# A decoder layer on one core: triangular solves placed on all four 64x64 tiles, decay sums shifted, values centred while they are turned

## The chip, the core and the metric

The kernel runs on one core of a Trainium2 chip: TensorE (matrix products into PSUM), VectorE, ScalarE and GpSimd (elementwise work), SyncE (issues the DMAs). The metric is the device time of one execution in microseconds (us), the median of the runs. Everything is float32. Products of large weights run as "split" products: a value is kept as a rounded high part and a low part, and hi x hi, hi x lo and lo x hi are summed.

## The reference

One layer for 256 tokens of width 2048. What bears on the change is the RWKV-7 mixer (16 heads of 64 columns):

```
w = -softplus(-(w0 + tanh(w_d) @ w_up)) - 0.5
decay = exp(-exp(w))                      # = exp(-DECAY * sigmoid(logit))
S_t = S_{t-1} * w_t + (S_{t-1} @ -kk_t) (kk_t * a_t)^T + v_t k_t^T ;  y_t = S_t r_t
mean = y.mean(-1); var = square(y - mean).mean(-1)      # per head
y = (y - mean) * rsqrt(var + eps) * gn_gain + gn_bias
out = (y + sum(r * k * r_k) * v) * g
```

Beside it stand a differential attention of 8 heads, one output projection, a LayerNorm, a squared-ReLU MLP (8192 wide) and a second LayerNorm.

## The kernel before

The program has five instruction streams, one for each engine, each written out in its order by hand. Semaphores tie them; there is no scheduler. Weights arrive as 1 MB slabs (128 x 2048 float32) in four rotating buffers `stage`. For each slab ScalarE rounds a high half (`hi`, tile `whi`), VectorE subtracts it for the low half (`lo`, tile `wlo`), and TensorE multiplies. Two slabs of halves are held, so `hi` of a slab waits until TensorE has used the slab two before it, and `lo` waits for `hi`.

The stages in order: the LoRA columns; decay and rate terms; the r, k, v columns of the projection (24 slabs, four rounds of three column groups); the attention's q and k (16 slabs, `q` = 0 to 15, in which the triangular solve is woven in); the attention's v with scores and softmax; transposes and chunk products; state passing; the group norm among output-projection products (`out_rows`); LayerNorm; MLP (128 slabs, some 730 us).

**Decay sums.** Tokens are in chunks of 64. For each of 8 blocks of 128 columns TensorE multiplies the decay sigmoids (`sig`) with two triangular 0/1 matrices side by side, 256 columns for each of two token tiles: the strict one gives the sum before a token, the inclusive one the sum up to it. The eight blocks pass through four PSUM banks (4 to 7). ScalarE takes exponentials of both (`kr`, with `e` = 0 and 1) and of the negated inclusive sum (`e2`). Between the sigmoids of the rates (`bt`) and the exponentials ScalarE also makes `hi` of slab 4 (`G_MIX + 1`). The rotary sines follow the exponentials.

**The solve.** There are 32 units (16 heads x 2 token tiles), each with two chunks, one in each half of the partitions. Groups of 8 units are solved in two streams (`st` 0 and 1) and two turns. For a turn, level 0 makes the matrices from PSUM (`AT`, and the starts of the inverse `TM` and its transpose `TT`); levels 1 to 5 each take an x product (factor `AT` times `TM`, 16 products of 64x64 over 64), a mask on VectorE into `XM`, a t product (32 products, `XM` with `TM`'s transpose both ways; 16 at level 5), and a copy back on ScalarE. `solve_at` puts level 0 at slab q = 1 and q = 8, and levels 1 to 5 at q = 3 to 7 and 10 to 14. Inside a slab the x products stand ahead of k steps 1 and 3, the t products ahead of steps 5 and 7.

A product whose inputs lie in partition half r and whose output lies in half o uses one quarter (64x64 tile) of the array, written (r to o) here. `halves_of` uses only (0 to 1) and (1 to 0), alternating; the t products of levels 1 to 4 use all four. A float32 product is two TensorE instructions, so `x32` in a row is 16 products.

**Turning.** `turned(i, bk)` makes eight 128x128 transposes; i = 2 and 3 are the values `v` (`krv` blocks 16 to 23 into `vtm`), i = 0 and 1 the keys, 4 and 5 `bt`, 6 and 7 `ki`.

**Group norm.** When y is complete (`copied(g)`, g = 0 to 3), TensorE sums each head with a block matrix of ones (`mean`, 128x512), VectorE subtracts the mean (`centred`), ScalarE squares, TensorE sums the squares, and root, reciprocal, spreading and gain follow.

Of the kernel before, what the change touches and what calls it, by code (L numbers as in the profile page):

```python
# [8 lines left out]
ALU = mybir.AluOpType  # L9
# [7 lines left out]
P = 128  # L17
# [88 lines left out]
def build(nc, t):  # L106

    ctx = ExitStack()
    with ctx:
# [9 lines left out]
        def sem(name):  # L119
# [43 lines left out]
        attT += [at("attT7", 22, [P, 3 * P])]  # L163
        otok = at("otok", 23, [P, TT_, RW])
# [5 lines left out]
        TM = at("TM", 16, [P, UNITS, C])  # L170
        TT = at("TT", 18, [P, UNITS, C])
        XM = [at("XM0", 24, [P, 8, C], byte=6144), at("XM1", 12, [P, 8, C], byte=5120)]

# [84 lines left out]
            "level_x", "level_x_masked", "level_products", "level_done"))  # L258
        s_rdx, s_rdm = sem("read_out_products"), sem("read_out_masked")
# [10 lines left out]
        s_mean, s_cen, s_gsq, s_var, s_sd, s_gn, s_gate, s_yg = (  # L270
            sem("gn_means"), sem("gn_centred"), sem("gn_squares"), sem("gn_vars"), sem("gn_roots"),
# [99 lines left out]
        def _(sp):  # L371
# [29 lines left out]
            sp.wait_ge(s_itemd, 2 * NB)  # L401
# [55 lines left out]
        def _(pe):  # L457
# [69 lines left out]
            for n in range(2 * NB):  # L527
                b, bk = n % NB, 4 + n % 4
                if n < 4:
                    pe.wait_ge(s_sig, n + 1)  # L530
                else:
                    pe.wait_ge(s_itemd, n - 3)
                if n < NB:
                    mm(ps[:, bk, 0:S], aup[64:128, P * b:P * b + P], wa[64:128, :]).then_inc(s_item, 1)
                else:
# [39 lines left out]
            def halves_of(bk, a0, b0):  # L575

                for c0 in range(2):
                    for j in range(4):
                        for c, jj, bank in ((c0, j, bk), (1 - c0, 4 + j, bk + 1)):
                            rows_ = chunk_rows(c)  # L580
                            last = mm(ps[chunk_rows(1 - c), bank, C * j:C * j + C], a0[rows_, jj, :], b0[rows_, jj, :])
                return last

            def level_x(st, turn, lev):
# [8 lines left out]
                else:  # L593
# [4 lines left out]
                    last = halves_of(bk, at_group(s), group(TM, s))  # L598
                last.then_inc(s_px[st], 1)

            def level_t(st, turn, lev):
                s, bk = STREAM[st][turn], 4 + 2 * st
                xm, tt = XM[st], group(TT, s)
                pe.wait_ge(s_xm[st], 6 * turn + lev + 1)
                if lev == 5:
                    last = halves_of(bk, xm, tt)
                else:
                    for j in range(8):
                        for r, out, bank, a0, b0 in ((0, 1, 0, tt, xm), (1, 0, 0, tt, xm), (0, 0, 1, xm, tt), (1, 1, 1, xm, tt)):
                            rows_ = chunk_rows(r)  # L610
                            last = mm(ps[chunk_rows(out), bk + bank, C * j:C * j + C], a0[rows_, j, :], b0[rows_, j, :])
# [134 lines left out]
            turned_read(0)  # L746
            turned(2, 0)
# [196 lines left out]
            def mean(g):  # L944
                pe.wait_ge(s_yc, g + 1)
                if g >= 2:
                    pe.wait_ge(s_cen, g - 1)
                mm(ps[:, g % 2, :], BD, yf[:, 2 * g:2 * g + 2, :]).then_inc(s_mean, 1)

# [150 lines left out]
        def _(act):  # L1100
# [48 lines left out]
            for n in range(2 * NB):  # L1149
                b, bk = n % NB, 4 + n % 4  # L1150
                if n == NB:
                    hi(G_MIX + 1, G_MIX + 1)
                act.wait_ge(s_item, n + 1)
                if n < NB:
                    A(bt[:, b, :], ps[:, bk, 0:S], ACT.Sigmoid, bias=col(V_A0, b)).then_inc(s_itemd, 1)
                else:
                    A(kr[:, b, :, :, :].rearrange("p a e q -> p (a e q)"), ps[:, bk, :], ACT.Exp, scale=-DECAY)
                    A(e2[:, b, :].rearrange("p (a q) -> p a q", a=TT_),
                      ps[:, bk, :].rearrange("p (a e q) -> p a e q", a=TT_, e=2)[:, :, 1, :],
                      ACT.Exp, scale=DECAY).then_inc(s_itemd, 1)  # L1160

            act.wait_ge(s_ang, 9)
            A(sinb[:, :], angt[0][:, :], ACT.Sin).then_inc(s_sin, 1)
            A(cosb[:, :], angt[2][:, :], ACT.Sin).then_inc(s_sin, 1)
# [6 lines left out]
            for j in range(NB // 2):  # L1171
                for c in range(3):
                    m = 3 * j + c
                    g = G_MIX + 2 * m
                    hi(g + 2, g + 2)
                    if c == 1:
# [899 lines left out]
```

## Time and profile before

| | us |
|---|---|
| median of 3 runs (1288.81, 1294.73, 1295.5) | 1294.73 |
| the profiled execution, own time | 1291.21 |
| its span | 1289.2 |
| TensorE matrix products busy | 1251.6 (97%) |
| TensorE weight loads busy | 1051.9 (82%) |
| VectorE / ScalarE / GpSimd busy | 756.4 / 574.7 / 72.1 |
| mean granted TensorE clock | 0.994 of full speed |

The span is the time from the first to the last instruction; the execution's own time is 2.0 us longer. All times inside the rows are counted from the span's start. `L459` is the helper through which nearly every matrix product is made, `L1102` the helper of every ScalarE activation, `L1449` the low half of a slab, so that the tile names tell which work it is.

### The profile page before, as it was taken

What the parts mean: (1) busy time and instruction counts of PE and PEld (TensorE: products, weight loads), DVE (VectorE), ACT (ScalarE), POOL (GpSimd) and SP (SyncE); (2) the same over time, 40 slices, a digit from 0 to 9 for tenths busy, and PEclk for the clock granted to TensorE, in tenths of its full rate; (3) what the DMA queues carried; (4) which work ended last, traced back from release to release, by engine and by line L of the source; (5) the groups of instructions that cost most, each with busy time, mean ns of one, the idle gap of its engine ahead of it and who ended that gap; (6) DMA issues with size and microseconds to landing.
All of it is one profiled execution on the core that took longest, in us unless ns stands there. A gap on an engine that the chain in (4) does not pass through costs nothing.

```text
span 1289.2 us, 23229 instructions
## 1 busy us (share of the span) xinstructions
PE 1251.6 (97%) x9624; PEld 1051.9 (82%) x9624; DVE 756.4 (59%) x797; ACT 574.7 (45%) x614; POOL 72.1 (6%) x42
## 2 busy tenths in 40 slices
PE   6999999999999999999999999999999999999995
PEld 6788888888778768888888888888888888888884
DVE  5478777454677245776555555555655555655557
ACT  4754444454665233433443334433444444444443
POOL 0021112000000000038000000000000000000000
PEclk9999999999999999999999999999999999999998
DMA  9254565232340243834555555555565555555541
GB/s 337 99 203 165 194 212 185 100 129 100 131 164 5 101 164 104 295 123 164 195 193 181 183 191 195 195 183 183 191 258 195 195 188 188 190 188 192 195 163 65
DMA packets 33505, 221.88 MB, mean 172 GB/s; under 512 B 4621, under 2 KB 5005, under 8 KB 7582
## 3 DMA queue, kind: packets, MB, share of 16 engines
q1 hardware_dynamic: 33438, 220.88, 49.5%
q8 instruction: 54, 0.88, 0.3%
q14 instruction: 13, 0.11, 0.0%
HBM read 218.77 MB, written 2.10 MB: 171 GB/s over the span
## 4 chain that ended last, share of the span: by engine, by line
PE 54%; DVE 1%; ACT 0%; issue 0%; DVEq 0%
PE ps L459 54%; DVE xres L1950 0%; DVE xres L1948 0%; DVE stats L1838 0%; DVE xres L1837 0%; ACT xres L1102 0%; DVE moments L1841 0%; DVE moments L1848 0%; ACT moments L1102 0%; DVE moments L1847 0%; DVEq L1831 0%
## 5 line engine op out<-in xcount | busy, mean ns | idle before, releaser
L1449 DVE TENSOR_TENSOR wlo<-stage,whi 128x2048 fp32r<-128x2048 f32 x186 | 436.0, 2344 | 387.7 <-ACT whi L1102 387.4
L459 PE MATMUL ps<-acts,whi 128*128 128x512 f32 (+1 forms) x1792 | 613.5, 391 | 15.3 <-DVE wlo L1449 13.1
L1102 ACT ACTIVATE whi<-stage 128x2048 fp32r<-128x2048 f32 x194 | 371.4, 1916 | 497.5 <-PE ps L459 494.3
L459 PE MATMUL ps<-acts,wlo 128*128 128x256 f32 (+1 forms) x1744 | 485.1, 278 | 0.0
L459 PEld LDWEIGHTS ps<-acts,whi 128*128 128x128 f32 x1792 | 333.7, 188 | 89.7 <-issue 20.1
L459 PEld LDWEIGHTS ps<-acts,wlo 128*128 128x128 f32 x1744 | 330.4, 189 | 1.9 <-issue 1.9
L459 PE MATMUL ps<-whi,shi 128*128 128x512 f32 x504 | 197.9, 393 | 0.0
L459 PE MATMUL ps<-wlo,shi 128*128 128x512 f32 x504 | 196.5, 390 | 0.0
L459 PE MATMUL ps<-whi,slo 128*128 128x512 f32 x504 | 196.2, 389 | 0.0
L459 PEld LDWEIGHTS ps<-whi,shi 128*128 128x128 f32 x504 | 94.5, 188 | 26.4 <-issue 6.1
L459 PEld LDWEIGHTS ps<-wlo,shi 128*128 128x128 f32 x504 | 94.6, 188 | 20.2
L459 PEld LDWEIGHTS ps<-whi,slo 128*128 128x128 f32 x504 | 94.7, 188 | 18.1
L459 PE MATMUL ps<-whi,oshi 128*128 128x512 f32 x128 | 53.2, 416 | 0.0
L459 PE MATMUL ps<-whi,oslo 128*128 128x512 f32 x128 | 50.4, 394 | 0.0
L459 PE MATMUL ps<-wlo,oshi 128*128 128x512 f32 x128 | 50.4, 394 | 0.0
L1803 DVE TENSOR_TENSOR slo<-hid,shi 128x512 fp32r<-128x512 f32 x64 | 43.8, 685 | 0.0
L459 PE MATMUL ps<-whi,acts 128*128 128x512 f32 x128 | 41.0, 402 | 0.0
L1102 ACT ACTIVATE shi<-hid 128x512 fp32r (+1 forms) x64 | 39.2, 613 | 1.1 <-PE ps L459 1.1
L1533 DVE TENSOR_TENSOR hs<-ps,hs 128x512 f32<-128x512 f32 x20 | 13.6, 679 | 44.5 <-ACT hs L1102 44.4
L1102 ACT ACTIVATE hs<-ps 128x512 f32<-128x512 f32 x20 | 12.0, 599 | 51.4 <-PE ps L459 51.4
L1988 POOL TENSOR_TENSOR acts<-x1f,acts 128x512 fp32r<-128x512 f32 x6 | 9.7, 1620 | 363.9 <-ACT acts L1102 363.9
L459 PEld LDWEIGHTS ps<-whi,oshi 128*128 128x128 f32 x128 | 24.2, 189 | 7.0 <-issue 2.0
(215 smaller groups left out, 996.9 us busy)
## 6 DMA issues: line engine op xcount, KB each, us to landing
stage<-w_ff SPq DMA_DIRECT2D x128, 1024.0 KB, 4.9
stage<-w_in SPq DMA_DIRECT2D x51, 1024.0 KB, 5.0
stage<-w_out SPq DMA_DIRECT2D x16, 1024.0 KB, 5.0
xstage<-xT SPq DMA_DIRECT2D x4, 512.0 KB, 7.2
xres<-x SPq DMA_DIRECT2D x1, 2048.0 KB, 7.9
gain<-ln_gain SPq DMA_DIRECT2D x2, 1024.0 KB, 6.9
bias<-ln_bias SPq DMA_DIRECT2D x2, 1024.0 KB, 9.0
out<-xres SPq DMA_DIRECT2D x8, 256.0 KB, 2.1
```

Of the source, the lines that this page charges most:

```text
L459: return pe.matmul(out, lhsT, rhs, start=start, stop=stop, skip_group_check=True)
L1102: return act.activation(out, in_, func, **kw)
L1449: TTn(wlo[k0 % NHL][:, :], stage[k0 % NST][:, :], f(whi[k0 % NHL][:, :]), ALU.subtract).then_inc(s_lo, 1)
L1533: TTn(hs[:, :, :], banks(2 * (m % 2), 2, 0, S), hs[:, :, :], ALU.add).then_inc(s_psum, 1)
L1803: TTn(slo[h][:, :, :], src, f(shi[h][:, :, :]), ALU.subtract).then_inc(s_alo, 1)
L1988: PT(actlo[:, ks, tok(a)], x1f[:, ks, tok(a)], f(acthi[:, ks, tok(a)]), ALU.subtract).then_inc(s_x1l, 1)
```

## The change

Four things are edited.

1. Decay sums: only the inclusive sums are made, four banks of two blocks each, 16 products of 128 columns. `kr` with `e` = 0 is taken from the same sums, read one column to the left; its first column in each chunk is set to 1 by a VectorE `memset`. There are three ScalarE exponentials for two blocks. Both halves of slab 4 are made on VectorE, and the sines are moved behind `hi` of slab 5.
2. Solve: units 0 to 3 of a group keep their output in the opposite half, units 6 and 7 in their own half, units 4 and 5 swap sides from level to level. The x products and the level-5 products go in squares of four that use all four tiles. Units 4 and 5 need their factor in both halves, so VectorE copies it (`AF`) at level 0. The t products of levels 1 to 4 write another layout, which ScalarE's two copies follow.
3. Values: `turned` 2 and 3 multiply by `centre` (identity minus 1/64 in each head's block) rather than transpose, so that y comes out centred; `mean` and `centred` are gone.
4. ScalarE makes `hi` of output slab 3 after the four squares, and the products of output slab 2 stand together.

```diff
@@ solve placement
+        def side_a(u, c, lev):
+            return c ^ (lev - 1) % 2 if u in (4, 5) else c
+        def side_s(u, c, lev):
+            return 1 - c if u < 4 else side_a(u, c, lev)
@@ decay sums, TensorE
-            for n in range(2 * NB):
-                b, bk = n % NB, 4 + n % 4
...
-                        last = mm(ps[:, bk, 256 * a:256 * a + 256], sig[:, a, P * b:P * b + P],
-                                  cst[:, C_SU:C_SU + 2 * P])
-                    last.then_inc(s_item, 1)
+            for p in range(NB // 2):
+                pe.wait_ge(s_itemd, 5 + p)
+                for b in (2 * p, 2 * p + 1):
                     for a in range(TT_):
+                        o = 256 * (b % 2) + P * a
+                        last = mm(ps[:, 4 + p, o:o + P], sig[:, a, P * b:P * b + P], IU)
+                last.then_inc(s_item, 1)
@@ solve, TensorE
-            def halves_of(bk, a0, b0):
-
-                for c0 in range(2):
-                    for j in range(4):
-                        for c, jj, bank in ((c0, j, bk), (1 - c0, 4 + j, bk + 1)):
-                            rows_ = chunk_rows(c)
-                            last = mm(ps[chunk_rows(1 - c), bank, C * j:C * j + C], a0[rows_, jj, :], b0[rows_, jj, :])
+            SQUARES = [[(u, c) for c in range(2) for u in (j, 4 + j)] for j in range(4)]
+
+            def x_products(st, s, bk, lev):
+                a0, b0 = at_group(s), group(TM, s)
+                for square in SQUARES:
+                    for u, c in square:
+                        a = side_a(u, c, lev)
+                        left = a0[chunk_rows(a), u, :] if a == c else AF[st][chunk_rows(a), u - 4, :]
+                        last = mm(ps[chunk_rows(side_s(u, c, lev)), bk + u // 4, C * (u % 4):C * (u % 4) + C], left,
+                                  b0[chunk_rows(a), u, :])
+                return last
+
+            def last_products(st, s, bk):
+                xm, tt = XM[st], group(TT, s)
+                for square in SQUARES:
+                    for u, c in square:
+                        rows_ = chunk_rows(side_s(u, c, 5))
+                        last = mm(ps[chunk_rows(c), bk + u // 4, C * (u % 4):C * (u % 4) + C], xm[rows_, u, :], tt[rows_, u, :])
+                return last
@@ values, TensorE
-                            last = pe.transpose(ps[:, bk + k, o:o + P],
-                                                TURNED_SRC[i // 2](4 * (i % 2) + 2 * k + b2, a), ID)
+                            if i // 2 == 1:
+                                last = mm(ps[:, bk + k, o:o + P], src, centre[:, :])
+                            else:
+                                last = pe.transpose(ps[:, bk + k, o:o + P], src, ID)
@@ group norm, TensorE
-            mean(0)
             pe.wait_ge(s_yc, 2)
-            for g in range(1, 4):
-                out_rows(G_OUT + 2, (g - 1,))
-                mean(g)
-            out_rows(G_OUT + 2, (3,))
+            out_rows(G_OUT + 2, range(4))
@@ decay exponentials, ScalarE
+                A(kr[:, two, :, 1, :].rearrange("p b a q -> p (b a) q"), ps[:, 4 + p, :].rearrange("p (m q) -> p m q", q=P),
+                  ACT.Exp, scale=-DECAY)
+                A(kr[:, two, :, 0, :].rearrange("p b a (c q) -> p (b a) c q", c=2)[:, :, :, 1:C], chunks[:, :, :, 0:C - 1],
+                  ACT.Exp, scale=-DECAY)
+                A(e2[:, two, :].rearrange("p b q -> p (b q)"), ps[:, 4 + p, :], ACT.Exp, scale=DECAY).then_inc(s_itemd, 1)
@@ slab 4, VectorE
-            lo(G_MIX + 1, G_MIX + 1)
+            dve.memset(kr[:, :, :, 0, 0::C].rearrange("p b a c -> p (b a) c"), 1.0)
+            g = G_MIX + 1
...
+            dve.tensor_copy(whi[g % NHL][:, :], stage[g % NST][:, :]).then_inc(s_hi, 1)
+            lo(g, g)
@@ level 0, VectorE
-                        last = dve.copy_predicated(by_head(group(TT, s))[out], mask(over8(M1T)[out]), bb[rows_])
+                        dve.copy_predicated(tt[out, 0], mask(over8(M1T)[out, 0]), bb[rows_, 0])
+                    dve.wait_ge(s_ax, 2 * turn + st + 1)
+                    for c in range(2):
+                        last = dve.tensor_copy(AF[st][chunk_rows(1 - c), :, :], at_group(s)[chunk_rows(c), 4:6, :])
@@ centring, VectorE
+            STT(centre[:, :], BD, -1.0 / HD, ID, ALU.mult, ALU.add).then_inc(s_centre, 1)
@@ group norm, VectorE
-                STT(y512, ps[:, g % 2, :], -1.0 / HD, y512, ALU.mult, ALU.add).then_inc(s_cen, 1)
```

The order of the instructions shows it at three places. On TensorE, the decay sums before (`sig` are the decay sigmoids, `cst` the triangular constants):

```order
L459 MATMUL ps<-wa_148,aup_63 128x256 [waits decay_sigmoid] x4
L459 MATMUL ps<-wa_148,aup_63 128x256 [waits rate_or_cumsum_done] x4
L459 MATMUL ps<-cst_144,sig_64 128x256 [waits rate_or_cumsum_done]
L459 MATMUL ps<-cst_144,sig_64 128x256
L459 MATMUL ps<-cst_144,sig_64 128x256 [waits rate_or_cumsum_done]
```

and the same place changed:

```order
L471 MATMUL ps<-wa_150,aup_63 128x256 [waits decay_sigmoid] x4
L471 MATMUL ps<-wa_150,aup_63 128x256 [waits rate_or_cumsum_done] x4
L471 MATMUL ps<-cst_146,sig_64 128x128 [waits rate_or_cumsum_done]
L471 MATMUL ps<-cst_146,sig_64 128x128 x3
L471 MATMUL ps<-cst_146,sig_64 128x128 [waits rate_or_cumsum_done]
```

Sixteen products of 256 columns in eight pairs become sixteen of 128 columns in four groups of four.

On VectorE, level 0 of one stream at q = 1, before:

```order
L1591 COPY_PREDICATED AT01_108<-cst_144,ps 128x512 [waits eyes_loaded_first_groups,level_x_stream0]
L1592 COPY_PREDICATED TM_110<-levc_107,ps 128x512
L1595 COPY_PREDICATED TT_111<-levc_107,ps 64x512 x2
```

and changed:

```order
L1637 COPY_PREDICATED AT01_109<-cst_146,ps 128x512 [waits eyes_loaded_first_groups,level_x_stream0]
L1638 COPY_PREDICATED TM_TT_111<-levc_108,ps 128x512
L1639 COPY_PREDICATED TM_TT_111<-levc_108,ps 128x256
L1642 COPY_PREDICATED TM_TT_111<-levc_108,ps 64x256 x2
L1645 COPY AF0_114<-AT01_109 64x128 [waits level_factors_ready]
L1645 COPY AF0_114<-AT01_109 64x128
```

Two operations of 512 columns become three of 256, and two copies of 128 columns are added.

On TensorE where y is complete, before (`yf` is y, `cst` the ones of a head):

```order
L459 MATMUL ps<-yf_132,cst_144 128x512 [waits y_copied]
L459 MATMUL ps<-whi1_54,oshi0_84 128x512 [waits diff_hi_ready,lo_ready,diff_lo_ready,hi_ready,y_copied]
L459 MATMUL ps<-whi1_54,oslo0_86 128x512
L459 MATMUL ps<-wlo1_56,oshi0_84 128x512
L459 MATMUL ps<-whi1_54,oshi0_84 128x512
L459 MATMUL ps<-whi1_54,oslo0_86 128x512
L459 MATMUL ps<-wlo1_56,oshi0_84 128x512
L459 MATMUL ps<-yf_132,cst_144 128x512 [waits y_copied]
```

and changed (`gsq` are the squares, the first product behind the slab):

```order
L471 MATMUL ps<-whi1_54,oshi0_84 128x512 [waits diff_hi_ready,lo_ready,diff_lo_ready,hi_ready,y_copied]
L471 MATMUL ps<-whi1_54,oslo0_86 128x512
L471 MATMUL ps<-wlo1_56,oshi0_84 128x512
L471 MATMUL ps<-gsq_136,sumg_133 16x256 [waits gn_squares,y_copied,norm_windows_loaded]
L471 MATMUL ps<-gsq_136,sumg_133 16x256
```

The four products on `yf` are gone (of the slab's 24 products the first three are shown).

## Rows read from the trace of the kernel before

**Rows 1.** Page, part 1: busy us (share of the span) x instructions of each engine.

```profile
PE 1251.6 (97%) x9624; PEld 1051.9 (82%) x9624; DVE 756.4 (59%) x797; ACT 574.7 (45%) x614; POOL 72.1 (6%) x42
```

**Rows 2.** Waits of PE: us in total, times, longest us.

```profile
PE ps L459 <- DVE wlo L1449: 13.1, 4, 11.5
```

**Rows 3.** Timeline, decay sums: start us, us, engine, line, op, count [idle before <-releaser].

```profile
34.99 0.29 DVE L1507 TENSOR_SCALAR angt<-angt 128x256 f32<-128x256 f32 x1
37.46 3.72 PE L459 MATMUL ps<-cst,sig 128*128 128x256 f32 x16
39.87 2.29 DVE L1449 TENSOR_TENSOR wlo<-stage,whi 128x2048 fp32r<-128x2048 f32 x1 [4.59 <-ACT whi L1102]
...
42.08 3.72 PE L459 MATMUL ps<-cst,sig 128*128 128x256 f32 x16 [0.90 <-ACT e L1102]
...
45.45 0.58 PE L459 MATMUL ps<-acts,whi 128*128 128x512 f32 x1
...
51.54 1.91 ACT L1102 ACTIVATE whi<-stage 128x2048 fp32r<-128x2048 f32 x1 [2.12 <-PE ps L459]
```

**Rows 4.** Timeline of PE, the attention's 128-column products and transposes.

```profile
391.90 2.84 PE L459 MATMUL ps<-vd,attT 128*128 128x128 f32 x24
394.58 1.04 PE L698 MATMUL ps<-cst,kr 128*128 128x128 f32 x8
395.45 1.04 PE L698 MATMUL ps<-cst,krv 128*128 128x128 f32 x8
...
397.39 1.09 PE L698 MATMUL ps<-cst,krv 128*128 128x128 f32 x8 [0.57 <-ACT kttm L1102]
398.90 1.06 PE L698 MATMUL ps<-cst,bt 128*128 128x128 f32 x8 [0.42 <-DVE vtm L1686]
```

**Rows 5.** Timeline of PE, solve: level 0's products at q = 1, x products at q = 3 and 4.

```profile
197.30 0.69 PE L459 MATMUL ps<-bt,kr 64*64 64x64 f32 x32
197.81 0.65 PE L459 MATMUL ps<-kr,bt 64*64 64x64 f32 x32
198.39 0.50 PE L459 MATMUL ps<-acts,whi 128*128 128x512 f32 x1
...
209.15 1.15 PE L459 MATMUL ps<-TM,AT 64*64 64x64 f32 x32
210.23 0.50 PE L459 MATMUL ps<-acts,whi 128*128 128x512 f32 x1
...
219.90 1.15 PE L459 MATMUL ps<-TM,AT 64*64 64x64 f32 x32
```

**Rows 6.** Window of one t product, PE alone: length, busy (x), PEclk, DMA, GB/s.

```profile
214.52:215.62 1.10, 1.10 (x66) 1.00 0.90 194
```

**Rows 7.** Lines by form, PE, 200 to 340 us: busy us, mean ns | idle before.

```profile
L459 PE MATMUL ps<-acts,whi 128*128 128x512 f32 x230 | 87.3, 416 | 1.3 <-DVE wlo L1449 1.3
```

**Rows 8.** Timeline of DVE, level 0 at q = 1.

```profile
199.34 0.75 DVE L1591 COPY_PREDICATED AT<-cst,ps 128x512 f32<-128x512 int32 x1
...
200.73 1.53 DVE L1595 COPY_PREDICATED TT<-levc,ps 64x512 f32<-64x512 int32 x2
202.29 0.76 DVE L1591 COPY_PREDICATED AT<-cst,ps 128x512 f32<-128x512 int32 x1
```

**Rows 9.** Timeline of ACT and PE, y copied and two head means of the group norm.

```profile
460.61 1.09 ACT L1102 ACTIVATE yf<-ps 128x512 f32<-128x512 f32 x2 [23.20 <-PE ps L459]
...
462.47 1.02 PE L459 MATMUL ps<-yf,cst 128*128 128x512 f32 x2
...
464.71 1.02 PE L459 MATMUL ps<-yf,cst 128*128 128x512 f32 x2
```

**Rows 10.** Windows: length, busy (x) of PE, PEld, DVE, ACT, POOL, PEclk, DMA, GB/s.

```profile
220.00:230.00 10.00, 10.00 (x221) 8.48 (x222) 6.17 (x7) 6.23 (x10) 0.00 (x0) 1.00 0.52 181
...
436.00:440.00 4.00, 2.15 (x144) 2.01 (x138) 1.29 (x2) 1.41 (x1) 0.00 (x0) 1.00 0.08 29
444.50:448.10 3.60, 3.60 (x44) 2.53 (x43) 1.29 (x2) 0.00 (x0) 0.00 (x0) 0.54 0.85 291
```

More of the change, by code:

```diff
@@ L163, in build @@
         attT += [at("attT7", 22, [P, 3 * P])]
+        centre = at("centre", 22, [P, P], byte=1536)
         otok = at("otok", 23, [P, TT_, RW])
@@ L525, in _ @@
                     mm(ps[:, 4 + 2 * a + q, :], wt[:, tok(a)], wup[:, 512 * q:512 * q + 512]).then_inc(s_z, 1)
-            for n in range(2 * NB):
-                b, bk = n % NB, 4 + n % 4
+            for n in range(NB):
                 if n < 4:
@@ new lines, in last_products, with t_products, inverse, transposed @@
+            def last_products(st, s, bk):
[5 more added lines that the diff above has]
+                return last
+            def t_products(st, s, bk, lev):
+                xm, tt = XM[st], group(TT, s)
+                def inverse(u, r):
+                    rows_, out = chunk_rows(r), chunk_rows(1 - r if u < 6 else r)
+                    o = C * u if u < 6 else C * (u - 2)
+                    return mm(ps[out, bk + u // 6, o:o + C], tt[rows_, u, :], xm[rows_, u, :])
+                def transposed(u, r):
+                    rows_, out = chunk_rows(r), chunk_rows(1 - r if u in (4, 5) else r)
+                    o = C * u if u < 4 else C * (u + 2) if u < 6 else C * u
+                    return mm(ps[out, bk + (u not in (4, 5)), o:o + C], xm[rows_, u, :], tt[rows_, u, :])
+                for u in range(4):
+                    inverse(u, 0)
+                    inverse(u, 1)
+                    transposed(u, 0)
+                    last = transposed(u, 1)
+                for u in (4, 5):
+                    for what in (inverse, transposed):
+                        for v in (u, u + 2):
+                            for r in range(2):
+                                last = what(v, r)
@@ L597, in level_x @@
                         pe.wait_ge(s_upd[st], 5 * turn + lev - 1)
-                    last = halves_of(bk, at_group(s), group(TM, s))
+                    last = x_products(st, s, bk, lev)
                 last.then_inc(s_px[st], 1)
@@ L602, in level_t @@
                 s, bk = STREAM[st][turn], 4 + 2 * st
-                xm, tt = XM[st], group(TT, s)
                 pe.wait_ge(s_xm[st], 6 * turn + lev + 1)
[L605 to L611, printed above, removed]
+                last = last_products(st, s, bk) if lev == 5 else t_products(st, s, bk, lev)
                 last.then_inc(s_ptx[st], 1)
@@ L1174, in _ @@
                     g = G_MIX + 2 * m
+                    if m == 0:
+                        act.wait_ge(s_hi, g + 2)
                     hi(g + 2, g + 2)
+                    if m == 0:
+                        sines()
                     if c == 1:
@@ L1204, in level_done @@
                 if lev < 5:
[L1205 to L1206 removed]
+                    o = 8 * C * s
+                    A(TM_TT[:, :, o:o + 256], banks(bk, 2, 0, 256), ACT.Copy)
+                    A(TM_TT[:, :, o + 256:o + 512].rearrange("p t (k q) -> p k t q", k=2),
+                      banks(bk, 2, 256, 512).rearrange("p k (t q) -> p k t q", t=2), ACT.Copy).then_inc(s_upd[st], 1)
                 else:
@@ L1340, in _ @@
             hi(G_OUT + 2, G_OUT + 2)
-            copied(0)
-            copied(1)
-            hi(G_OUT + 3, G_OUT + 3)
-            copied(2)
-            copied(3)
+            for g in range(4):
+                copied(g)
             for g in range(4):
                 squared(g)
+            hi(G_OUT + 3, G_OUT + 3)
             hi(G_OUT + 4, G_OUT + 4)
@@ L1788, in rwkv_lo @@
                 TTn(oslo[1][:, bl, :], yt[:, bl, :], f(oshi[1][:, bl, :]), ALU.subtract).then_inc(s_olo[1], 1)
-            centred(0)
             lo(G_OUT + 3, G_OUT + 3)
-            for g in range(1, 4):
-                centred(g)
             lo(G_OUT + 4, G_OUT + 4)
```

71 lines of the change are left out of this document (32 added, 39 removed).

## The prediction

> **What bounds the kernel now.** I read the busy shares first, then what TensorE waits for, then the timeline at each edited place, TensorE ahead of the engines that serve it. TensorE's products are busy 1251.6 of 1289.2 us, VectorE 59%, ScalarE 45% [rows 1]. TensorE's waits for a low half are 13.1 us in all, of which 11.5 is the one before its first product [rows 2]. So TensorE is the bound nearly everywhere, and a microsecond taken off its stream comes off the end, unless VectorE or ScalarE becomes late. There are three places where TensorE does wait near the edits: 0.90 us at the decay sums for ScalarE's exponentials [rows 3], 1.3 us in the solve, all of it for low halves of slabs [rows 7], and 0.57 and 0.42 us among the turned values [rows 4]. The first shrinks with the edit, in the second every added VectorE operation counts in full, the third can swallow added work. Everything behind the group norm (some 790 us) is not touched and only starts earlier.
>
> **Decay sums.** TensorE starts on them at 37.46 and is on the first projection slab at 45.45 [rows 3]: 7.99 us, which is 32 instructions of 256 columns in two blocks of 3.72 and the wait between. Now there are 16 products of 128 columns, 32 instructions. The pace of such instructions with full weights is in the attention: 24 take 391.90 to 394.58, 0.112 us each [rows 4]. 32 x 0.112 = 3.6 us. All four groups have a free bank once the rates are read, so no wait stands inside. Gain 8.0 - 3.6 = 4.4 us. What must be in time: both halves of slab 4. VectorE is free from 35.3 [rows 3]; the low half takes 2.29 us there, the high half by a copy has no row, and I bound it by 0 and by the same 2.29. Even then both are done by 35.5 + 4.6 = 40.1, and slab 4 is only needed after slab 3, which TensorE begins at 37.5 + 3.6 = 41.1. ScalarE loses a 1.9 us `hi` and keeps its exponentials: twelve of 512 columns against eight of 512 and eight of 256, 6144 columns either way. Its next `hi` (slab 5) waits for TensorE anyway, 2.12 us at 51.54 [rows 3], and the sines are moved behind it, where VectorE needs them only when slab 4 is through. I find nothing late. Bounds of the gain: 4.0 (0.4 of start-up) and 4.4.
>
> **Solve.** An x product is 32 instructions on two tiles and takes 209.15 to 210.23, 1.08 us. What would 32 instructions on four tiles take? Level 0's products use all four: the first 32 take 197.30 to 197.81, 0.51, the second, with the change back to full width, 0.58 [rows 5]. A t product on four tiles, 64 instructions, is 1.10 us [rows 6]: twice the work in the time of one x product. Taking its 1.10 as 64 steps plus about 0.15 for the change over, 32 steps come to 0.63. So 0.58 to 0.63; I take 0.60 and a gain of 0.48 each. There are 2 turns x 2 streams x 5 levels = 20 x products and 4 of level 5 in squares: 24 x 0.48 = 11.5 us (10.8 to 12.0). The t products of levels 1 to 4 keep their count and their four tiles: 0. ScalarE's two copies carry the same elements: 0.
>
> What must be in time here: a slab with solve work shrinks from 10.75 us (209.15 to 219.90, x product to x product [rows 5]) to 9.8. VectorE's mask of stream 1 stands behind a `lo` and ahead of the rotary work, and nothing on TensorE waits for a mask: the view of waits names none, and the only idle time of 200 to 340 us stands before slab products, 1.3 us, for low halves [rows 7]. In 220 to 230 us VectorE is busy 6.2 and ScalarE 6.2 of 10 [rows 10]. Both have about 2 us in hand for each slab, and 0.5 us of it goes before the t products. Cost 0.
>
> Against it stands level 0. VectorE does it in 199.34 to 202.29, 2.95 us for a stream [rows 8], and what follows is the low half for which TensorE waits, at q = 1 to 3 and again at q = 8 to 10; so additions count. Two 512-column operations of 1.53 become three of 256; one 512 is about 0.53 of columns and 0.2 of fixed time by the 0.75 there, so 256 is 0.27 + 0.15 to 0.2, three about 1.3. Two copies of 128 columns have no row: between 0.1 and 0.3 each. Together 1.5 to 1.9 against 1.5: 0 to +0.4, I take +0.1, times 4 = +0.4 us (0 to 1.4).
>
> **Values.** A transpose is one instruction: eight take 394.58 to 395.45, 0.109 each [rows 4]. As products they are two each at 0.112, so eight take 1.79 instead of 0.87. Two calls add 1.8 us of work. The first starts at 395.45 as before and ends 0.9 later; the wait of 0.57 in front of the second goes, then the second adds 0.9, and the wait of 0.42 in front of the turned `bt` goes. 1.84 - 0.57 - 0.42 = 0.85; the copies that ended those waits move by a little with the products, but the last copy of the values was queued behind a reduction on VectorE and hardly moves. I take +0.7 us (0.4 to 1.8). The `centre` tile is one VectorE operation while VectorE waits for TensorE: 0.
>
> The Trainium skill (TensorE: Matmul & The Clock Gate, Terms) says that transpose mode makes float32 four times faster. The trace gives a factor of two, 0.109 against 2 x 0.112 [rows 4]. By the page a product would be 0.44, sixteen would add 5.2 us rather than 1.8, and the gain would be 3.4 us smaller; the rows decide.
>
> **Group norm.** A mean and six slab products take 462.47 to 464.71 = 2.24 us [rows 9]. A mean is two instructions of 512 columns, as much as four of 256, which are 3.72 / 16 = 0.23 each [rows 3], so 0.9, with the tail of the group in it; I take 0.86, which leaves 0.23 for each slab product. Four means: 3.4 us. Behind it the squares must be in time. The four copies of y and the squares on ScalarE no longer wait for VectorE, and slab 3's `hi` stands after them; TensorE has 24 products (5.5 us) of slab 2 to do meanwhile. ScalarE's four copies and four squares, at 1.09 for two [rows 9], are some 4.4 us from 460.6, the `hi` and `lo` of slab 3 are 1.9 and 2.3 more [rows 3]: 469 us. TensorE comes to slab 3 no sooner than 462.5 + 5.5 + 3.7 for the sums of squares (16 instructions of 256 columns) = 471.7. Cost 0; bounds of the gain 2.5, where slab 3 were a microsecond late, and 3.5.
>
> **The sum.** -4.4 - 11.5 + 0.4 + 0.7 - 3.4 = -18.2 us. The profiled execution took 1291.2 us, so 1273.0 by its own clock. It lies between the timed runs of 1288.8 and 1295.5, whose median is 1294.7, so these would give 1276.5. I take the mean of the four executions, 1292.6, as the base: 1274.4, say 1274.5 us. Half a per cent, about what a measurement of this kernel can tell from no change, is 6.5 us: under 1288.3 is faster.
>
> **Rivals.**
> 1. *The squares do not overlap.* The Trainium skill (TensorEngine Tiling, Gotcha 1) says that different row tiles cannot access the same PSUM bank at the same time, and each square sends two row halves into one bank. If TensorE serialised such pairs, an x product would stay at 1.08. For it: the edit does put (0 to 1) and (1 to 0) of one square into one bank, on different output halves. Against it: the t products do so too and run 64 instructions in 1.10 [rows 6]. The gain would be 18.2 - 11.5 = 6.7, time 1286. A chance of 0.06.
> 2. *The level chain becomes the bound.* If the mask or the copy of stream 1 came after its reader in each of the ten slabs, half of the solve's gain would be given back: 12.5 us of gain, 1280. For it: VectorE and ScalarE handle everything in a fixed order behind `hi` and `lo`. Against it: no such wait now, and 2 us in hand. 0.10.
> 3. *TensorE runs out of instructions (slower).* Where the 64x64 products stand densest, 436 to 440 us, TensorE is busy 2.15 of 4.00 us at 144 instructions, with no engine to wait for; after such holes its clock is at the lower level, 1.2 GHz, for most of 3.6 us (granted 0.54) [rows 10]. The new x products put 32 instructions into 0.6 us. If each of the 24 calls met a hole of 1.3 us, that would be +31 and the time 1305; it decides from 18.2 / 24 = 0.76 us a call. Against it: slabs with solve work run 221 instructions in 10 us without a hole [rows 10] and would run 224 in 9.8, and the t products are as dense as the new ones. 0.03.
> 4. *The clock moves.* The same stretch at 444.5 costs 3.6 x (1 - 0.5) = 1.8 us; work ahead of it moves by 16 us, and it may go, or another may come: 1.8 either way, inside the range.
> 5. *The edits do little*, since something hidden holds the old pace at the decay sums and the norm as well: 1288 to 1292, 0.03.
>
> **Numbers.** The forecast has 0.78, its own range 1268 to 1281: gains from 15 to 20.5, and bases from 1288.8 to 1295.5. Rival 2 ends at 1280 to 1283, rival 1 at 1286, rival 3 above 1290. I give 1268 to 1283. Faster: 0.78 + 0.10 + 0.05 of rival 1 = 0.93. Within half a per cent: 0.01 + 0.03 = 0.04. Slower: 0.03.
>
> **What would show it.** Decay sums: 32 instructions of 128 columns in one block of 3.6 us, the first slab product at about 41, no wait between. Solve: the `TM,AT` group of 32 over 0.6 us, distance from one x product to the next of its stream about 9.8 us where it was 10.75; the wait for low halves between 1.3 and 2 us. Values: groups of 16 on `centre`, turned `bt` less than 1 us later against its neighbours. Norm: no products on `yf`, 24 slab products in one piece, `gsq` straight behind. It would be wrong if an x product keeps 1.08 us, if TensorE shows new holes with no releaser, if VectorE's level 0 grows by 0.5 us or more for a stream, or if ScalarE's slab 5 `hi` comes after TensorE's need.

## The result and the profile after

The changed kernel takes 1280.57 us (median of 6 runs, 1276.29 to 1282.53) against 1294.55 for the one before (6 runs): a ratio of 0.989, 95% interval 0.987 to 0.992. Forecast were 1274.5 us, range 1268 to 1283. The profiled execution took 1276.29 us with a span of 1274.5, so the span is 14.7 us shorter than the 1289.2 of before; the forecast was 18.2.

The busy line of the page, which answers to [rows 1]:

```profile
PE 1236.8 (97%) x9632; PEld 1038.0 (81%) x9632; DVE 756.9 (59%) x808; ACT 572.2 (45%) x609; POOL 69.8 (5%) x42
```

TensorE's products are 14.8 us shorter at nearly the same count, and that is the change of the span: TensorE still is the bound. Its waits (us in total, times, longest), beside [rows 2]:

```profile
PE ps L471 <- DVE wlo L1490: 15.0, 3, 11.6
PE ps L471 <- issue: 4.3, 3, 2.1
```

The waits for low halves grew from 13.1 to 15.0 us. The timeline says which ones. First the decay sums, beside [rows 3] (start us, us, engine, line, operation, count, idle before):

```profile
37.26 2.29 DVE L1490 TENSOR_TENSOR wlo<-stage,whi 128x2048 fp32r<-128x2048 f32 x1
...
38.26 3.84 PE L471 MATMUL ps<-cst,sig 128*128 128x128 f32 x32
...
41.85 0.48 PE L471 MATMUL ps<-acts,whi 128*128 128x512 f32 x1
```

One block from 38.26 to 41.85, no wait in it and slab 4's low half done at 39.6. Now TensorE at q = 3, where [rows 5] had the first x product at 209.15:

```profile
206.27 0.47 PE L471 MATMUL ps<-acts,whi 128*128 128x512 f32 x1 [1.96 <-DVE wlo L1490]
...
207.13 0.76 PE L471 MATMUL ps<-TM_TT,AT 64*64 64x64 f32 x32
207.81 0.80 PE L471 MATMUL ps<-acts,whi 128*128 128x512 f32 x1
...
228.27 0.69 PE L471 MATMUL ps<-TM_TT,AT 64*64 64x64 f32 x32
```

Before, TensorE waited 0.45 us for a low half at q = 3 and 0.88 at q = 9; now the second is 1.42 (two rows of the kernel before, then one of the changed kernel):

```profile
208.28 0.47 PE L459 MATMUL ps<-acts,whi 128*128 128x512 f32 x1 [0.45 <-DVE wlo L1449]
...
276.96 0.47 PE L459 MATMUL ps<-acts,whi 128*128 128x512 f32 x1 [0.88 <-DVE wlo L1449]
```

```profile
271.46 0.47 PE L471 MATMUL ps<-acts,whi 128*128 128x512 f32 x1 [1.42 <-DVE wlo L1490]
```

The x product at 228.27 is what was forecast (0.62 us to its successor's start, where it was 1.08), but the one at 207.13 runs behind a wait of 1.96 us, and its neighbour, a slab product of 512 columns, has 0.80 us where 0.40 is usual. The windows show why (length; busy (x) of PE, PEld, DVE, ACT, POOL; PEclk; DMA; GB/s):

```profile
204.00:207.00 3.00, 1.04 (x6) 0.60 (x4) 2.59 (x2) 2.94 (x5) 0.00 (x0) 1.00 0.00 0
207.00:208.00 1.00, 1.00 (x35) 0.76 (x34) 0.96 (x3) 1.00 (x1) 0.00 (x0) 0.81 0.77 131
208.00:209.00 1.00, 1.00 (x3) 0.86 (x4) 1.00 (x2) 0.44 (x1) 0.00 (x0) 0.50 0.87 328
...
211.00:212.00 1.00, 1.00 (x35) 0.89 (x28) 0.76 (x2) 0.00 (x0) 0.00 (x0) 0.98 0.04 16
```

TensorE idled for two of the first three microseconds, and then the granted clock is 0.50, the level of 1.2 GHz, from 208 to 211. Before there is no fall in the solve. The low half comes late because VectorE's level 0 is longer. Here is all of it at q = 1 for stream 0, the copies of stream 1, and GpSimd beside it; [rows 8] is its counterpart:

```profile
195.81 0.75 DVE L1637 COPY_PREDICATED AT<-cst,ps 128x512 f32<-128x512 int32 x1
196.45 0.73 DVE L1638 COPY_PREDICATED TM_TT<-levc,ps 128x512 f32<-128x512 int32 x1
197.09 0.43 DVE L1639 COPY_PREDICATED TM_TT<-levc,ps 128x256 f32<-128x256 int32 x1
197.53 0.93 DVE L1642 COPY_PREDICATED TM_TT<-levc,ps 64x256 f32<-64x256 int32 x2
198.47 1.60 DVE L1645 COPY AF<-AT 64x128 f32<-64x128 f32 x2
...
202.74 0.46 DVE L1645 COPY AF<-AT 64x128 f32<-64x128 f32 x2
```

```profile
197.21 1.29 POOL L2024 TENSOR_TENSOR bt<-bt,e  x1 [0.17 <-POOL kr L2022]
198.47 1.28 POOL L2025 TENSOR_TENSOR ki<-ki,e  x1
```

The same two copies take 1.60 us for stream 0, beside GpSimd's product of `ki`, and 0.46 for stream 1, when GpSimd is through. Taken singly, it is one copy that is long; it ends 0.09 us after the product of `ki` (199.75), and the next takes 0.22:

```profile
198.47 1.37 DVE L1645 COPY AF<-AT 64x128 f32<-64x128 f32 x1
199.85 0.22 DVE L1645 COPY AF<-AT 64x128 f32<-64x128 f32 x1
```

The three predicated copies, which read PSUM, are at 0.43 to 0.93 in both streams. Level 0 of both streams takes 7.42 us (195.81 to 203.23) where it took 5.91: stream 0 has 1.34 us more and stream 1 0.17.

The values go in two blocks on `centre` with no wait before them or before the turned `bt` (beside [rows 4]), and at the group norm ScalarE makes four squares and then `hi` of slab 3 (beside [rows 9]):

```profile
384.60 1.95 PE L471 MATMUL ps<-centre,krv 128*128 128x128 f32 x16
...
386.71 1.95 PE L471 MATMUL ps<-centre,krv 128*128 128x128 f32 x16
388.50 1.04 PE L744 MATMUL ps<-cst,bt 128*128 128x128 f32 x8
```

```profile
451.43 2.21 ACT L1138 ACTIVATE gsq<-yf 128x512 f32<-128x512 f32 x4
453.51 1.93 ACT L1138 ACTIVATE whi<-stage 128x2048 fp32r<-128x2048 f32 x1
```

From marks on TensorE's timeline (before / after): decay sums to slab 3, 7.99 / 3.59 us; decay sums to the first x product, 171.69 / 168.87; from there to the turned values, 186.30 / 177.47; values to the first chunk products, 7.12 / 7.54; from there to the squares' sums, 68.97 / 64.74. Those are -4.40, then +1.58 (the second stretch holds the first), -8.83, +0.42 and -4.23: 15.5 us gained, of which a start 0.8 us later (38.26 for 37.46) leaves the 14.7 of the span. That start lies anywhere from 37.46 to 38.55 in the eleven traces of this document, whichever edits they have, so it is chance. Behind the squares both need 817.6 us.

### The profile page after: what moved, and what is told of

Same layout as the page of the kernel before. It is cut to its first block, busy times and chain, and to the rows that moved or that the text cites. A ratio compares the mean times of both kernels' runs of the same rounds, so it can differ in the third digit from the quotient of the medians.

```text
span 1274.5 us, 23249 instructions
## 1 busy us (share of the span) xinstructions
PE 1236.8 (97%) x9632; PEld 1038.0 (81%) x9632; DVE 756.9 (59%) x808; ACT 572.2 (45%) x609; POOL 69.8 (5%) x42
## 4 chain that ended last, share of the span: by engine, by line
PE 54%; DVE 1%; ACT 0%; issue 0%; DVEq 0%
PE ps L471 54%; DVE xres L1994 0%; DVE xres L1992 0%; DVE stats L1882 0%; DVE xres L1881 0%; ACT xres L1138 0%; DVE moments L1885 0%; DVE moments L1892 0%; ACT moments L1138 0%; DVE moments L1891 0%; DVEq L1875 0%
## 5 line engine op out<-in xcount | busy, mean ns | idle before, releaser
L471 PEld LDWEIGHTS ps<-whi,slo 128*128 128x128 f32 x504 | 94.7, 188 | 18.2
L1138 ACT ACTIVATE TM_TT<-ps 128x512 f32<-128x512 f32 x36 | 19.8, 596 | 45.2 <-PE ps L471 45.2
```

Source lines behind the costliest of these rows:

```text
L471: return pe.matmul(out, lhsT, rhs, start=start, stop=stop, skip_group_check=True)
L1138: return act.activation(out, in_, func, **kw)
```

## The experiments

All ran with five rounds but the last (three). The kernel before had a median of 1290.35 us beside the first four, of 1295.25 beside the next four, and of 1295.35 beside the last. Executions of one and the same kernel differ by up to 11 us (1288.65 to 1299.12 for the kernel before, 1268.92 to 1280.07 for `af_scalar`), of which some 6 us arise in the MLP, behind everything edited here (last section); so the traces' marks decide between variants, and medians only where they are far apart. Marks scatter too, each being one execution: the chunk products up to the squares' sums need 63.4 to 66.2 us in the eight traces without means and 67.2 to 69.9 in the three with them.

**The three parts alone.** `sums_only` has edit 1, `solve_only` edit 2, `values_only` edits 3 and 4, each on the kernel before.

```diff
 sums_only:   -  mm(ps[:, bk, 256 * a:256 * a + 256], sig[...], cst[:, C_SU:C_SU + 2 * P])
              +  mm(ps[:, 4 + p, o:o + P], sig[...], IU)
 solve_only:  +  SQUARES = [[(u, c) for c in range(2) for u in (j, 4 + j)] for j in range(4)]   (and AF)
 values_only: -  mean(g); centred(g)
              +  mm(ps[:, bk + k, o:o + P], src, centre[:, :])
```

> The kernel before with the decay-sum edit alone (inclusive sums only, shifted exponentials, slab 4 on VectorE, sines later). Theory 1 (each edit brings on TensorE what its stream loses, and all the shortfall of 3.5 us lies at level 0 of the solve): 4.4 us less than before, ratio 0.9966. Theory 2 (part of this gain is given back further on, where the projection slabs follow sooner on each other): 2 to 3.5 us less, and a wait of TensorE for a low half in the projection that before did not have.

Measured: 1286.62 us (12 runs, 1284.32 to 1292.19), ratio 0.996 (0.994 to 0.998). The decay sums to slab 3 take 3.60 us, so the term is 4.4, and the sign of the second theory is not there: no wait for a low half that the kernel before did not have (13.1 us in all in both). The interval of the ratio, 2.5 to 7.9 us, holds both theories.

> The kernel before with the solve edit alone (three placements, squares on four tiles, factor copies on VectorE at level 0). Theory 1 (x products at 0.6 us give 11.5 us; VectorE's level 0 grows by more than was priced, 1.5 us at q = 1 beside GpSimd's work and 0.5 at q = 8; the wait that it makes lets TensorE's clock fall for 3.6 us, 1.8 more): 11.5 - 2.0 - 1.8 = 7.3 to 7.7 us less, ratio 0.994; the rows show a wait of about 1.9 us at q = 3 with the granted clock at 0.5 behind it. Theory 2 (the growth at q = 1 comes from the earlier start of the whole program and is not there with the solve edit alone): 11 us less, ratio 0.9915, no clock fall near q = 3.

Measured: 1284.09 us (9 runs), ratio 0.994 (0.992 to 0.996). The waits at q = 3 and q = 9 are 1.98 and 1.59 us where `sums_only` has 0.59 and 0.89, and the clock falls behind the first (0.60 in 212 to 216 us). So the solve's edit alone brings both.

> The kernel before with the centring edit alone (values multiplied by the centring matrix as they are turned, no means, slab 3's high half later). Theory 1: the means bring 3.4 to 3.6, the turned values cost 0.4 (two waits absorb the rest of 1.8): 3.1 us less, ratio 0.9976. Theory 2 (the centred products cost their full 1.8 us): 1.7 us less, ratio 0.9987.

Measured: 1293.34 us (12 runs, 1286.96 to 1296.01), ratio 1.001 (0.999 to 1.003): inconclusive as a time. In the trace the values cost +0.4 us (7.54 for 7.12) and the stretch that held the means, from slab 2's first product to the squares' sums, is 3.55 us shorter (7.03 for 10.58), so some 3 us are gained, less than the scatter.

**Where the side factor is copied.** `af_scalar` makes the copies on ScalarE behind level 0 instead of on VectorE in it; TensorE waits for them only at level 2, which first reads them.

```diff
-   for c in range(2): last = dve.tensor_copy(AF[st][...], at_group(s)[...])      # in level 0
...
+   act.wait_ge(s_ax, 2 * turn + st + 1)                                          # ScalarE, at level 1
+   for c in range(2): last = A(AF[st][...], at_group(...)[...], ACT.Copy)
```

> The changed kernel with the four factor copies (AF) on ScalarE at q = 3 and q = 10, where ScalarE waits for TensorE, in place of VectorE at level 0. Theory 1 (the copies on VectorE's path make the waits for low halves and with them the clock fall): the wait at q = 3 falls from 1.96 us to 0.2 or less, the one at q = 8 to 10 from 1.42 to about 0.4, the clock stays at 2.4 GHz there; 4.5 us less than the changed kernel, ratio to before 0.986. Theory 2 (the clock falls there for another reason, for instance because TensorE's work in the solve is now made of short products on four tiles): the waits go but the clock still falls, 2.8 us less than the changed kernel, ratio 0.9873.

Measured: 1274.59 us (6 runs, 1268.92 to 1280.07), ratio 0.987 (0.983 to 0.991). No wait at q = 3, 0.48 us at q = 9, clock 1.00 all through the solve. The second theory, by which the clock would fall without the waits, is out.

A second job ran it again beside the changed kernel itself and `af_late`, which leaves the copies on VectorE but puts those of both streams behind level 0 of both.

```diff
     if work: level_x(1, *work)
+    if work and not work[1]: side_factors(work[0])      # VectorE: four copies, both streams
```

> The changed kernel once more, beside its variants on one chip. By my theory the trace again has a wait for a low half of about 1.96 us at q = 3 and of 1.42 at q = 9, with the granted clock at the lower level for some 3 us behind the first, and an x product at about 0.6 us; median 1280 to 1283. If these were chances of one execution, the wait at q = 3 is back at 0.5 to 0.9 here and no fall of the clock stands in the solve.

> The two copies of the side factor stay on VectorE but stand behind level 0 of both streams; TensorE takes them by a semaphore of their own at level 2. Theory 1 (VectorE's operations stretch while GpSimd runs its products of the same time): stream 0's copies no longer stand beside GpSimd's and take 0.46 a stream as stream 1's do, level 0 of both streams with copies is about 1.1 us shorter at q = 1, the wait at q = 3 falls from 1.96 to about 0.8, the clock does not fall in the solve, and the wait at q = 9 stays at 1.4; the time is 2 to 3 us below the changed kernel's. Rival (the copies cost what they cost, wherever they stand): the wait at q = 3 stays within 0.3 of 1.96 and the time does not move.

> The variant with the side factor copied on ScalarE, once more beside the changed kernel itself on one chip. By theory 1 it is 2 to 5 us faster than the changed kernel (the wait of 1.96 us and the fall of the clock behind it go, 1 us goes at q = 9): 1274 to 1278. If its earlier lead was the chip's, the two agree within 1 us.

Measured: `after_again` 1276.13 us (1273.55 to 1280.94), `af_late` 1274.60 (1273.96 to 1279.69), `af_scalar_again` 1274.89 (1269.08 to 1276.96), six runs each, ratios 0.987, 0.986 and 0.985. The median of `after_again` lies below the 1280 to 1283 expected of it, and 4.4 us below the first six runs of the very same kernel; its wait, its fall of the clock and its x products came as expected. TensorE at q = 3 and 9 in `after_again`, then in `af_late`, then at q = 9 in `af_scalar_again`, which has no wait at q = 3:

```profile
205.88 0.47 PE L471 MATMUL ps<-acts,whi 128*128 128x512 f32 x1 [1.98 <-DVE wlo L1490]
...
271.11 0.47 PE L471 MATMUL ps<-acts,whi 128*128 128x512 f32 x1 [1.41 <-DVE wlo L1490]
```

```profile
204.33 0.47 PE L471 MATMUL ps<-acts,whi 128*128 128x512 f32 x1 [0.86 <-DVE wlo L1492]
...
268.12 0.47 PE L471 MATMUL ps<-acts,whi 128*128 128x512 f32 x1 [1.47 <-DVE wlo L1492]
```

```profile
265.85 0.47 PE L471 MATMUL ps<-acts,whi 128*128 128x512 f32 x1 [0.32 <-DVE wlo L1501]
```

And VectorE in `af_late`, at a time when GpSimd's product of `ki` (to 198.92) is over:

```profile
200.32 0.95 DVE L1653 COPY AF<-AT 64x128 f32<-64x128 f32 x4
```

Four copies take 0.95 us behind GpSimd's work, where two took 1.46 to 1.60 beside it. In `after_again` the first of the two began just ahead of the product of `ki` (198.22 to 199.58) and took 0.22; the second met it and lasted until 0.09 us after its end:

```profile
198.21 0.22 DVE L1645 COPY AF<-AT 64x128 f32<-64x128 f32 x1
198.44 1.23 DVE L1645 COPY AF<-AT 64x128 f32<-64x128 f32 x1
```

`solve_only`, `pair_order` and `one_tile` have the same pair, 0.22 and 1.23. With nothing but the copies' place moved, the wait at q = 3 is 0.86, as forecast by the first theory, and 1.47 at q = 9, where no GpSimd work stands near. The rival (a copy costs the same wherever it stands) falls. The windows behind q = 3, of `after_again` and then of `af_late`:

```profile
207.00:211.00 4.00, 4.00 (x72) 3.18 (x62) 3.93 (x4) 1.06 (x1) 0.00 (x0) 0.58 0.66 246
```

```profile
207.00:211.00 4.00, 4.00 (x109) 3.24 (x108) 3.02 (x3) 0.13 (x1) 0.00 (x0) 1.00 0.64 197
```

The fall of the clock went with the wait. It stood behind q = 3 in every trace that waited 1.80 to 1.98 us there (five, of four kernels) and in none of the six that waited 0.86 or less; waits of 1.41 to 1.59 at q = 9 brought none. The length of a pause alone does not settle it: among the chunk products `sums_only` has a hole of 1.85 us and no fall. From the x product at q = 3 to the one at q = 5 `after_again` needs 21.18 us and `af_scalar_again` 19.68, so a fall costs 1.5 us. From level 0's first product on TensorE to the first product on the attention's values (`vd`) behind the solve, `after_again`, `af_late` and `af_scalar_again` take 189.76, 187.46 and 185.41 us.

As whole times the three are not told apart: their medians lie within 1.5 us, so neither the 2 to 3 us expected of `af_late` nor the 2 to 5 of `af_scalar_again` showed. `af_late`'s 2.3 us are lost again at the chunk products (to the sums of the squares it needs 264.71 us, `after_again` 264.55), where its clock is low for 12 us rather than for some 4, behind a hole of 2.23 us without a releaser. `after_again` has a hole of 2.07 us at the same place, and its clock fell only behind the next one, of 1.01 us; why is open. `af_scalar` keeps its gain in its two traces (262.20 and 259.88 us to the same mark, where the changed kernel's two have 265.81 and 264.55) and has the lowest execution, 1268.9; it beats the kernel before clearly and the changed kernel by its traces, though not by its median beyond doubt.

**How many tiles in turn.** `pair_order` and `one_tile` change the order of the sixteen products of an x product (and of the last level) and nothing else.

```diff
-   SQUARES = [[(u, c) for c in range(2) for u in (j, 4 + j)] for j in range(4)]                 # four tiles in turn
+   SQUARES = [[(u, c) for u in range(4 * h, 4 * h + 4) for c in range(2)] for h in range(2)]    # pair_order: two
+   SQUARES = [[(u, c) for u in range(4 * h, 4 * h + 4)] for h in range(2) for c in range(2)]    # one_tile: one
```

> The changed kernel with the products of an x product in another order: first the eight whose tiles lie off the diagonal, then the eight on it, so that only two tiles alternate at any time, as in the kernel before. The placements, the sums and the values are unchanged. If four tiles in turn are what shortens the x product, it is back at 1.08 us and 24 x 0.48 = 11.5 us of the gain are lost: some 1290 to 1293, with the waits at q = 3 and 9 near nothing. If the placement alone or the fewer masks did it, the x product stays at 0.6 and the time at 1280 to 1283.

> The changed kernel with each x product's sixteen products sorted by tile: four in a row on one tile, then four on the next. So far 32 instructions took 0.63 us with four tiles in turn and 0.91 with two in turn (first the pair off the diagonal, then the pair on it). Theory A (a tile holds its next instruction back and other tiles fill that time, so the pace goes with the number of tiles in turn): one tile at a time is well slower than two, about 0.15 + 2 x 0.76 = 1.7 us an x product; 24 of them lose some 25 us against the changed kernel, about 1300 to 1303, unless they cover the waits for low halves. Rival B (only the changes between the pairs matter, or the four tiles are needed for another reason): about 0.9 again and 1283 to 1286.

Measured: `pair_order` 1284.6 us (6 runs, 1280.77 to 1289.73), ratio 0.992 (0.990 to 0.995); `one_tile` 1296.78 (10 runs, 1293.04 to 1303.21), ratio 1.004 (1.001 to 1.007). One x product at full clock in the changed kernel, in `pair_order` and in `one_tile`:

```profile
228.27 0.69 PE L471 MATMUL ps<-TM_TT,AT 64*64 64x64 f32 x32
```

```profile
228.38 0.98 PE L471 MATMUL ps<-TM_TT,AT 64*64 64x64 f32 x32
```

```profile
230.69 1.54 PE L471 MATMUL ps<-TM_TT,AT 64*64 64x64 f32 x32
```

(The modelled end overlaps the next product by 0.07; from start to next start it is 0.62, 0.91 and 1.47 us.) In the first two it is the same at every level (two of the 24 in `pair_order` took 1.02 and 1.06). In `one_tile` it is 1.47 at levels 1, 3 and 5 but 1.25 at levels 2 and 4, where units 4 and 5 have swapped sides, so that the last eight products stand on one tile for two, on the other for four and on the first again for two. One at level 2, from its start to that of the slab product behind it:

```profile
222.46 0.79 PE L471 MATMUL ps<-TM_TT,AT 64*64 64x64 f32 x13
...
223.71 0.50 PE L471 MATMUL ps<-acts,whi 128*128 128x512 f32 x1
```

The three times fit 0.35 + 1.12 / n for n tiles in turn: 0.63, 0.91, 1.47. My reading is that a tile holds back its own next product, 0.035 us an instruction, and that others fill that time. The formula is a fit of two numbers to three points and holds for these x products only: for a t product, 64 instructions on four tiles, it would give 0.91 where 1.09 is measured, and level 0's first 32 took 0.51. My 1.08 for two tiles was too high and my 1.7 for one as well, since I took 0.15 as the fixed part; the waits at q = 3 and 9, expected near nothing in `pair_order`, were still 1.80 and 1.58. TensorE's marks follow: from the first x product to the turned values the three need 177.47, 184.62 and 196.09 us, 7.1 and 18.6 more than the changed kernel, against 24 x 0.28 = 6.7 and 16 x 0.84 + 8 x 0.63 = 18.5. The lowest executions are 1273.6, 1280.8 and 1293.0.

So with the layout kept, the order is worth 0.28 of the 0.455 us that an x product gained. The other 0.17 stands between two in turn before (1.08) and two in turn here (0.91), and its cause is open. The order of the PSUM banks is a rival that was not tried by itself: the kernel before alternates two banks from product to product, and so does the changed kernel, while `pair_order` and `one_tile` stay in one bank for eight products. Between these two only the tiles differ; between `pair_order` and the changed kernel the banks differ as well.

## Why the prediction was right, point by point

The forecast stands in its direction and within its range, and the mechanism of the three gains held; the price of level 0 did not. It gave 3.5 us too much (18.2 for 14.7 of span). Level 0 has 1.65 us of that and the fall of the clock that it set off 1.5; the x products have 0.6 and the later start 0.8. Against these stand 0.3 at the values, 0.15 at the norm and 0.7 among the chunk products, which nothing edited and which scatter by that much.

That the time lies within the range is in part luck. The terms' own bounds add up to a gain of 14.1 to 19.5 us, not the 15 to 20.5 that the prediction states, and the measured gains, 14.0 by the medians and 14.7 by the spans, lie below 15. The time is inside, 0.4 us from the end of the forecast's own 1268 to 1281, because the range was also made of bases up to 1295.5. The same kernel had a median of 1276.13 in the later job. Two of the signs named beforehand also came out against it: level 0 grew by 1.34 us for stream 0, where 0.5 was to count as wrong, and the waits for low halves behind the first product are 3.4 us, where 1.3 to 2 were expected.

- *Decay sums*, 4.4 forecast: 4.40 measured, and 0.112 us an instruction held.
- *Solve, the products*, 11.5 forecast: 1.08 - 0.625 = 0.455 each, 24 of them 10.9. 0.60 was a little too low; the bracket from level 0's 0.58 and the t product's 0.63 held; the slab takes 9.84 us (half of 19.68) at full clock where 9.8 was forecast. No mask or copy of the level chain became late (rival 2), and the squares overlap (rival 1). That rival came from the Trainium skill (TensorEngine Tiling, Gotcha 1), by which different row tiles should not share a bank at one time; here squares that do so take 0.62 us, and eight products in one bank that change the row tile every time, with different output halves, still go at the pace of 0.91 in `pair_order` where 1.47 is measured tile by tile. So these traces do not bear it out for products with different output halves.
- *Solve, level 0*, +0.4 forecast (0 to 1.4): the wait at q = 3 grew from 0.45 to 1.96 and that at q = 9 from 0.88 to 1.42, together +2.05. **This is the term that failed.** The step was "two copies of 128 columns have no row: between 0.1 and 0.3 each". The duration is right, 0.22, where nothing is beside it; beside GpSimd's product one copy took 1.23 to 1.37, until that product was over. I bounded it from rows of VectorE alone and never asked what GpSimd did in those microseconds, though in the trace of before `lo` was already stretched there, 3.20 us for the usual 2.29:

```profile
196.22 3.20 DVE L1449 TENSOR_TENSOR wlo<-stage,whi 128x2048 fp32r<-128x2048 f32 x1
```

```profile
195.98 1.29 POOL L1977 TENSOR_TENSOR bt<-bt,krv  x1 [28.55 <-DVE krv L1524]
197.23 3.35 POOL L1978 TENSOR_TENSOR kr<-kr,krv  x1
```

  The rest is the choice within the bracket: at q = 8 a stream pays 1.36 for three predicated copies and 0.46 for the plain ones against 1.53, +0.29, inside the 0 to 0.4 but not the 0.1 that I took; two streams of it are 0.58, beside 0.54 more wait at q = 9.
- *The clock*, rival 4, "1.8 either way": the old fall stayed among the chunk products (0.61 in 432 to 436 us), and a new one came at q = 3, 1.5 us. It was no chance of position: it stood there in all five traces with that wait and in none without it, so it belonged into the price of level 0. The 1.96 us of wait cost 1.5 us more through the clock.
- *Values*, +0.7 (0.4 to 1.8): +0.42. The two waits of 0.57 and 0.42 went, and what stood behind them was not late. That leaves 0.85 by the prediction's sum; of the 0.43 less, 0.22 is that the second eight transposes of the values took 1.09 us from their start to the idle time behind them, where 0.87 is usual, and the rest is not separated. The Trainium skill's factor of four for transposes (TensorE: Matmul & The Clock Gate, Terms) would have shown here as 3 us more and did not: 16 instructions take 1.78 us against 0.87 for eight transposes, twice.
- *Group norm*, 3.4: 3.55 from slab 2's first product to the squares' sums (10.58 before, 7.03 now). `hi` of slab 3 ends at 455.4 and its low half at 457.8, while TensorE has been on the 16 instructions of the squares' sums only since 456.88: covered as said.
- *Sum*: 4.4 + 10.9 + 3.55 - 0.42 - 2.05 - 1.5 = 14.9 against 15.5 between the marks. The 0.6 left is about the chunk products' 0.7, which no term holds.

## What to carry to other kernels

A new operation's duration is not its price: look at which engines run beside it and how long similar work takes there (here a copy of 0.22 us cost what was left of another engine's 1.3 us), and at what the added wait does to TensorE's clock. Work added ahead of the low half of a weight slab belongs on the engine with slack (`af_scalar`), if its first reader is further down; behind that half on the same engine was not tried. Small products on quarter tiles should be issued with all four tiles in turn; taking two in turn instead cost 0.28 us for sixteen of them, and one at a time 0.84.

## What the runs showed of the hardware

- *VectorE beside GpSimd.* In these traces the operations that read SBUF alone became longer and the one that reads PSUM did not. A copy of 64x128 takes 0.22 us by itself; the one that met GpSimd's product of `ki` ended 0.08 to 0.09 us after it in all five traces that have it there, at 1.23 to 1.37 us. `lo` takes 3.19 us at 192.69, begun 0.24 us behind GpSimd's product of `bt` (192.45 to 193.74, that of `kr` follows), and 2.28 at 203.84. A predicated copy of 128x512 that reads PSUM takes 0.73 in both cases.
- *A plain copy* (`CAST` in the changed kernel's trace) of 128x2048 from SBUF to SBUF on VectorE takes 1.19 us where the subtraction of the same size takes 2.29; I had bounded it by 0 and 2.29.
- *A second pace of the MLP.* At a granted clock of 1.00 throughout and with no wait, some executions run the first MLP product slower. The kernel before and `sums_only`, 700 to 900 us, by line and form (busy us, mean ns | idle before):

```profile
L459 PE MATMUL ps<-acts,whi 128*128 128x512 f32 x578 | 200.4, 391 | 0.0
L459 PE MATMUL ps<-acts,wlo 128*128 128x256 f32 x578 | 161.8, 280 | 0.0
```

```profile
L459 PE MATMUL ps<-acts,whi 128*128 128x512 f32 x567 | 200.4, 399 | 0.0
L459 PE MATMUL ps<-acts,wlo 128*128 128x256 f32 x567 | 159.2, 281 | 0.0
```

  That is 0.346 against 0.353 us for a pair, 2% over some 300 us, or 6 us. `sums_only` had its marks 6 us ahead when it came to the MLP and still ended at 1289.1 us beside 1289.2; its fastest execution, 1284.3, shows the gain of 4.4. Of eleven traces three had the slower pace (`sums_only`, `pair_order`, `one_tile`). It does not follow the edits; its cause is open.
- *Holes without a releaser* stand where 64x64 products are densest. One of 1.85 to 2.29 us is in all eleven traces at one place, in front of a product on `um` that starts 35.3 to 36.7 us behind the first chunk product; smaller ones, 0.2 to 1.6 us, come and go from trace to trace. Nothing here removed them.
